# Expert rows scattered by choice and token in a two-layer diffusion trunk: stores, combination loads, gate rows and modulation moved between engines

## The reference

```python
DEPTH = 2; D_MODEL = 1024; SEQ = 128; DEC_SEQ = 512          # 640 tokens in all
N_EXPERTS = 32; TOP_K = 4; EXPERT_FF = 128; SHARED_FF = 256; ROUTE_SCALE = 2.5

def moe_ffn(h, p):
    t = h.reshape(-1, d)
    s = jax.nn.sigmoid((t @ p["w_router"]).astype(jnp.float32))
    _, idx = lax.top_k(s + p["b_router"].astype(jnp.float32), TOP_K)
    sel = jnp.take_along_axis(s, idx, axis=-1)
    w = sel / jnp.sum(sel, axis=-1, keepdims=True) * ROUTE_SCALE
    gates = jnp.einsum("nk,nke->ne", w, jax.nn.one_hot(idx, N_EXPERTS))
    hg = jnp.einsum("nd,edf->nef", t, p["w_e_gate"])
    hu = jnp.einsum("nd,edf->nef", t, p["w_e_up"])
    routed = jnp.einsum("nef,efd->nd", jax.nn.silu(hg) * hu * gates[:, :, None], p["w_e_down"])
    shared = (jax.nn.silu(t @ p["w_s_gate"]) * (t @ p["w_s_up"])) @ p["w_s_down"]
    return (routed + shared).reshape(bn, l, d)

def trunk_layer(x, cvec, p, layer, ctx=None):
    mods = jax.nn.silu(cvec) @ p["w_ada"] + p["b_ada"]
    sh1, sc1, g1, sh2, sc2, g2 = jnp.split(mods[:, None, :], 6, axis=-1)
    h = rmsnorm(x, p["g_pre1"]) * (1.0 + sc1) + sh1
    ...                                    # differential attention, SSD scan, neighbourhood attention
    mix = (ga * (o_da @ p["w_br_da"]) + gs * (o_ssm @ p["w_br_ssm"]) + gn * (o_na @ p["w_br_na"])) @ p["w_out"]
    x = x + g1 * rmsnorm(mix, p["g_post1"])
    h2 = rmsnorm(x, p["g_pre2"]) * (1.0 + sc2) + sh2
    x = x + g2 * rmsnorm(moe_ffn(h2, p), p["g_post2"])
```

## Time and profile before

| | us |
|---|---|
| median of 3 runs | 2956.16 (2955.13 to 2956.25) |
| the profiled execution's own time | 2964.08 |
| its span | 2962.3 |
| granted TensorE clock, mean | 0.935 |
| DMA, mean | 153 GB/s, 452.96 MB |
| stores of `y` in both loops | 76 |

### The profile page before, as it was taken

One profiled execution on the slowest core, in us unless ns is written; L12 is line 12 of the kernel. 1 busy time (PEld: TensorE's weight loads), 2 busy tenths in 40 slices (PEclk: granted clock), 3 DMA queues, 4 the chain that ended last, 5 costly groups with the idle time before them and its releaser, 6 DMA issues. The chain is left out here.

```text
span 2962.3 us, 32617 instructions
## 1 busy us (share of the span) xinstructions
PE 2582.0 (87%) x11924; PEld 1666.3 (56%) x11924; DVE 980.1 (33%) x1955; ACT 605.9 (20%) x1362; POOL 348.0 (12%) x338
## 2 busy tenths in 40 slices
PE   4999969879999989999829998986999998899993
PEld 2445634456457645677615565545656764577771
DVE  1414301463006334222164242136301633522226
ACT  2221100340014012122132121025001401212221
POOL 0005100011001100111220150000200110011113
PEclk8999989999988999999969999989998999999997
DMA  8441086100542030799853101710033103089996
GB/s 307 143 143 36 29 313 245 36 1 29 187 143 48 29 111 36 289 378 380 304 193 123 64 29 36 294 64 1 29 127 95 42 29 118 29 331 379 378 350 219
DMA packets 189030, 452.96 MB, mean 153 GB/s; under 512 B 30732, under 2 KB 52340, under 8 KB 188916
## 3 DMA queue, kind: packets, MB, share of 16 engines
q1 hardware_dynamic: 139668, 306.49, 29.1%
q10 hardware_dynamic: 31968, 82.02, 7.4%
q0 software_dynamic: 17280, 62.92, 5.8%
HBM read 362.00 MB, written 89.39 MB: 152 GB/s over the span
## 5 line engine op out<-in xcount | busy, mean ns | idle before, releaser
L221 PE MATMUL ps<-hT,ring 128*128 128x512 f32 x896 | 414.4, 617 | 13.7 <-PEq L2756 12.4
L2262 PEld LDWEIGHTS ps<-mixT,ring 128*128 128x128 f32 x2496 | 284.5, 192 | 96.9 <-issue 96.9
L2262 PE MATMUL ps<-mixT,ring 128*128 128x128 f32 x2496 | 297.1, 277 | 35.7 <-PE ps L2278 34.0
L221 PEld LDWEIGHTS ps<-hT,ring 128*128 128x128 f32 x896 | 173.2, 198 | 233.3 <-issue 233.1
L230 PE MATMUL ps<-ring,hT 128*128 128x512 f32 x480 | 212.3, 600 | 8.4 <-PEq L1177 7.4
L1215 POOL TENSOR_TENSOR mix_S<-ring 128x512 f32<-128x512 f32 x16 | 25.2, 1577 | 1197.5 <-POOLq L1352 630.3
L2148 PE MATMUL ps<-ring,mixT 128*128 128x512 f32 x320 | 144.0, 611 | 21.6 <-PEq L2756 21.6
L230 PEld LDWEIGHTS ps<-ring,hT 128*128 128x128 f32 x480 | 91.3, 192 | 122.5 <-issue 120.3
L2278 PE MATMUL ps<-ring,ex_hid 128*128 128x512 f32 x304 | 149.5, 614 | 0.0
L1264 PE MATMUL ps<-late,ring 128*128 128x320 f32 x512 | 144.4, 440 | 5.6 <-PEq L1701 2.5
L1264 PEld LDWEIGHTS ps<-late,ring 128*128 128x128 f32 x512 | 98.0, 193 | 49.8 <-issue 10.9
(11 more groups left out here) (404 smaller groups left out, 3605.0 us busy)
## 6 DMA issues: line engine op xcount, KB each, us to landing
ring<-in_w_e_gate SPq DMA_DIRECT2D x78, 512.0 KB
ring<-in_w_e_up SPq DMA_DIRECT2D x78, 512.0 KB
ring<-in_w_e_down SPq DMA_DIRECT2D x78, 512.0 KB
y_rows<-out_gpost ACTq DMA_DIRECT2D x76, 512.0 KB, 6.3
ring<-in_w_in SPq DMA_DIRECT2D x18, 2048.0 KB, 8.4
y_rows<-hT SPq DMA_DIRECT2D x12, 2560.0 KB, 31.1
ring<-in_w_gate SPq DMA_DIRECT2D x12, 2048.0 KB, 9.7
mixT<-in_w_ada ACTq DMA_DIRECT2D x8, 2048.0 KB, 9.4
```

What stands on the lines that cost most here:

```text
L221: pe.matmul(lat, wide[:, k, c], hT[:, k, CTX:TOK], start=(k == 0), stop=(k == kt_n - 1))
L2262: ins = pe.matmul(ps[:, 2 + b, g * P:(g + 1) * P], ew[:, k, :], xT[:, b, k, :], start=(k == 0), stop=(k == KT - 1))
```

## The change

Each result row now goes to a place of its own, choice x 640 + token, and rows of empty slots are not written. POOL scatters them with an indirect DMA in the loop; ScalarE's store is gone, and so are the filler stores and their wait. The gather leaves out empty slots too (an index beyond the bound). The table is therefore built from choice and token, and split on VectorE into `m.table` (the row to read) and `m.dest` (the row to write). Two small scatters of two rows each go into spare rows first and count for `y_stored`.

In the combination the rows are plain loads of 128 consecutive rows, issued by SP. The first row of each token goes through TensorE: `diag`, the identity scaled by the gate, times the row, added to the shared product in PSUM; VectorE adds the other three. The gate rows are loaded by ScalarE's queue near the start of the expert loop, the next layer's mods by SP at the start of `stage_tail`. ScalarE modulates all eight blocks.

```diff
@@ stage_da, sync: the filler stores
-            spare = UNROLL * (MAX_TURNS - MIN_TURNS)
-            for a in range(0, spare, TILES):
-                n = min(TILES, spare - a)
-                sp.dma_start(cx.y_rows[UNROLL * MIN_TURNS + a:...], cx.hT ...).then_inc(sem("rows_filled"), 16)
@@ stage_tail, sync
             load_mods(cx, sp, L, 1, mods, sem("mods_in"))
+            if L + 1 < DEPTH:
+                load_mods(cx, sp, L + 1, 0, m.mods, sem("co_mods_in"))
@@ stage_tail, gpsimd
                 pool.indirect_dma_start(xg[:, b, :], None, cx.h_rows,
-                                        bass.IndirectOffsetOnAxis(ap=index[:, b:b + 1], axis=0)).then_inc(...)
+                                        bass.IndirectOffsetOnAxis(ap=index[:, b:b + 1], axis=0), bounds_check=TOK - 1,
+                                        oob_is_err=False).then_inc(sem(f"xg_ready{b}"), 16)
+            def scatter(n, i):
+                b = n % 2
+                pool.wait_ge(sem("y_low"), at(n + 3, i))
+                pool.wait_ge(sem("y_high"), at(n + 3, i))
+                pool.tensor_copy(goal[:, b:b + 1], m.dest[:, bass.ds(at(n, i), 1)]).then_inc(sem("goal_ready"), 1)
+                pool.wait_ge(sem("goal_ready"), at(n + 1, i))
+                pool.sem_inc(sem("pool_go"), 1)
+                pool.indirect_dma_start(cx.y_rows, bass.IndirectOffsetOnAxis(ap=goal[:, b:b + 1], axis=0), y[:, b, :],
+                                        None, bounds_check=TOP_K * TOK - 1, oob_is_err=False).then_inc(
+                    sem(f"y_stored{b}"), 16)
             pool.wait_ge(sem("table_known"), 1)
+            for b in range(2):
+                pool.indirect_dma_start(cx.y_rows, bass.IndirectOffsetOnAxis(ap=goal[0:2, b:b + 1], axis=0), y[0:2, b, :],
+                                        None).then_inc(sem(f"y_stored{b}"), 16)
             gather(0)
             gather(1)
             with pool.Fori(0, count) as i:
                 for n in range(2, UNROLL + 2):
                     gather(n, i)
+                    scatter(n - 2, i)
+            for b in range(2):
+                pool.wait_ge(sem(f"y_stored{b}"), count * (16 * UNROLL // 2) + 16)
@@ stage_tail, scalar
             turned(0)
             shared(1)
+            act.wait_ge(sem("table_known"), 1)
+            act.wait_ge(sem("rows_stored"), 16 * TILES)
+            load_gate(cx, act, L, 1, m.gpost, m.gbias, m.ggain, sem("co_gains"))
             silu_up(0)
...
-                    act.wait_ge(sem("y_low"), at(n + 2, i))
-                    act.wait_ge(sem("y_high"), at(n + 2, i))
-                    act.dma_start(cx.y_rows[bass.ds(at(n - 1, i), 1)]..., y[:, b, :]).then_inc(sem(f"y_stored{b}"), 16)
@@ stage_tail, vector: what the table holds
-                                            token[:, t:t + 1], ALU.is_equal, ALU.mult)
+                                            place_of[:, n:n + 1], ALU.is_equal, ALU.mult)
-                dve.scalar_tensor_tensor(out=m.slot_of[:, k, :], ...)
-            dve.tensor_copy(m.table[:, :], ps[:, 3, 0:TABLE]).then_inc(sem("table_known"), 1)
+            known = ps[:, 3, 0:TABLE]
+            for b in range(2):
+                dve.tensor_scalar(goal[:, b:b + 1], col, float(TOP_K * TOK + 2 * b), None, ALU.add)
+            dve.tensor_scalar(tab[:, 0, :], known, 0.0, NO_ROW, ALU.is_equal, ALU.mult)
+            step(dve, dve.tensor_scalar(tab[:, 2, :], known, float(TOK), None, ALU.is_gt))
+            for k in range(2, TOP_K):
+                step(dve, dve.scalar_tensor_tensor(out=tab[:, 2, :], in0=known, scalar=float(k * TOK), ...))
+            step(dve, dve.scalar_tensor_tensor(out=tab[:, 1, :], in0=known, scalar=-1.0, in1=tab[:, 0, :], ...))
+            dve.scalar_tensor_tensor(out=m.table[:, :], in0=tab[:, 2, :], scalar=-float(TOK), in1=tab[:, 1, :], ...)
+            dve.tensor_copy(m.dest[:, :], tab[:, 1, :]).then_inc(sem("table_known"), 1)
@@ stage_combine
-        @block.gpsimd
-                pool.indirect_dma_start(yg[:, n % BUFS, :], None, cx.y_rows..., m.slot_of[:, k, t:t + 1] ...)
...
+                n = t * TOP_K
+                if t == 0:
+                    pe.wait_ge(sem("co_diag"), 1)
+                pe.wait_ge(sem(f"yg_ready{n % BUFS}"), 16 * (n // BUFS + 1))
+                for h in range(2):
+                    ins = pe.matmul(ps[:, 2 * (t % 3) + h, :], diag[:, t, :], yg[:, n % BUFS, h * SEC:(h + 1) * SEC],
+                                    start=False, stop=True)
...
-                for k in range(4):           # ScalarE; blocks 4 to 7 were VectorE's modulate(t), now gone
+                for k in range(KT):
...
-            load_gate(cx, sp, L, 1, gpost, old[:, 3, :], old[:, 4, :], sem("co_gains"))
+            def load_rows(t):
+                for k in range(TOP_K):
+                    n = t * TOP_K + k
+                    if n >= BUFS:
+                        sp.wait_ge(sem("yg_used"), n - BUFS + 1)
+                    sp.dma_start(yg[:, n % BUFS, :], cx.y_rows[k * TOK + t * P:k * TOK + (t + 1) * P, :]).then_inc(...)
+            load_rows(0)
+            load_rows(1)
             if more:
-                load_mods(cx, sp, L + 1, 0, mods, sem("co_mods_in"))
                 load_section(cx, sp, L + 1, 0)
             for t in range(TILES):
+                if t + 2 < TILES:
+                    load_rows(t + 2)
                 sp.wait_ge(sem("x2_ready"), t + 1)
...
+            for t in range(TILES):
+                ins = dve.tensor_scalar(diag[:, t, :], cx.ident, m.gates[:, 0, t:t + 1], None, ALU.mult)
+            ins.then_inc(sem("co_diag"), 1)
...
-                for k in range(TOP_K):
+                for k in range(1, TOP_K):
@@ trunk
-    cx.y_rows = nc.dram_tensor("y_rows", [UNROLL * MAX_TURNS, P, D], F32, kind="Internal").ap()
+    cx.y_rows = nc.dram_tensor("y_rows", [TOP_K * TOK + 4, D], F32, kind="Internal").ap()
```

More of the change, by code:

```diff
@@ L58 @@
 TABLE = UNROLL * MAX_TURNS + 4
+NO_ROW = 4096.0
 OFF = {}
@@ L2023, in sb @@
             return st.enter_context(nc.sbuf_tensor(f"{name}_{L}", shape, dt))
-        xn = sb("out_xn", [P, TILES, D])
+        xn = m.rest
         mods = Mods(sb("out_mods", [P, 184]))
@@ L2030, in stage_tail @@
         br = sb("route_br", [P, NE])
-        iota = sb("route_iota", [P, P + TILES + 1])
+        iota = sb("route_iota", [P, P + N_CHOICE + 1])
         s = sb("route_s", [P, TILES, NE])
@@ L2055, in stage_tail @@
         y = gpost
+        m.gpost = cx.late[:, :, :].rearrange("p a b -> p (a b)")[:, 0:2 * D].rearrange("p (g d) -> p g d", g=2)
+        m.gbias, m.ggain = m.rest[:, 0, :], m.rest[:, 1, :]
         row = iota[:, 0:P]
-        token = iota[:, P:P + TILES]
-        col = iota[:, P + TILES:P + TILES + 1]
+        place_of = iota[:, P:P + N_CHOICE]
+        col = iota[:, P + N_CHOICE:P + N_CHOICE + 1]
         block = st.enter_context(nc.Block())
@@ L2504, in _ @@
             for k in range(TOP_K):
-                dve.scalar_tensor_tensor(out=m.slot_of[:, k, :], in0=chosen[:, k, 1, :], scalar=float(P),
-                                         in1=chosen[:, k, 0, :], op0=ALU.mult, op1=ALU.add)
                 dve.tensor_copy(m.gates[:, k, :], chosen[:, k, 2, :])
@@ L2509, in _ @@
             dve.wait_ge(sem("table_mm"), 1)
-            dve.tensor_copy(m.table[:, :], ps[:, 3, 0:TABLE]).then_inc(sem("table_known"), 1)
+            known = ps[:, 3, 0:TABLE]
[4 more added lines that the diff above has]
+            for k in range(2, TOP_K):
+                step(dve, dve.scalar_tensor_tensor(out=tab[:, 2, :], in0=known, scalar=float(k * TOK), in1=tab[:, 2, :],
+                                                   op0=ALU.is_gt, op1=ALU.add))
+            step(dve, dve.scalar_tensor_tensor(out=tab[:, 1, :], in0=known, scalar=-1.0, in1=tab[:, 0, :], op0=ALU.add,
+                                               op1=ALU.add))
+            dve.scalar_tensor_tensor(out=m.table[:, :], in0=tab[:, 2, :], scalar=-float(TOK), in1=tab[:, 1, :],
+                                     op0=ALU.mult, op1=ALU.add)
+            dve.tensor_copy(m.dest[:, :], tab[:, 1, :]).then_inc(sem("table_known"), 1)
             def turned(n, i=0):
@@ L2527, in _ @@
             dve.sem_inc(sem("y_high"), 2)
-            for b in range(2):
-                dve.sem_inc(sem(f"y_stored{b}"), 16)
             dve.wait_ge(sem("experts_known"), 1)
@@ L2557, in stage_combine @@
         fs = sb("co_fs", [P, 6, TILES])
-        gpost = sb("co_gpost", [P, 2, D])
-        mods = Mods(sb("co_mods", [P, 184]))
+        gpost = m.gpost
+        diag = m.rest[:, 2, 0:TILES * P].rearrange("p (t q) -> p t q", q=P)
         spare = cx.ring[:, 1:SLOTS, :].rearrange("p s n -> p (s n)")
@@ L2563, in stage_combine @@
         block = st.enter_context(nc.Block())
-        @block.gpsimd
-        def _(pool):
-            for n in range(N_CHOICE):
-                t, k = n // TOP_K, n % TOP_K
-                if n >= BUFS:
-                    pool.wait_ge(sem("yg_used"), n - BUFS + 1)
```

(17 more changed lines are left out.)

43 lines of the change are left out of this document (14 added, 29 removed).

## The result

The changed kernel took 2935.19 us (median of 4 runs, 2934.94 to 2938.14) beside 2956.2 for the kernel before (4 runs), a ratio of 0.9938 (95% interval 0.9918 to 0.9959): 21.0 us less, where 41.9 were forecast. Later, beside the last experiments, it took 2942.28 (12 runs, 2930.68 to 2950.22) beside 2952.56 (17 runs), 0.9962 (0.9948 to 0.9977): 10.3 us less. All runs together have 2938.4 (16) against 2952.4 (63), so 14.0 us. The forecast of 2914.3 was wrong, and its range ended at 2935. The profiled execution of after took 2938.14 (span 2936.3).

A forecast was written before the change was run, and what follows sets the result against it. TensorE, busy 2582.0 of 2962.3 us, bounds the kernel; edits pay where it stands still or another engine ends a stage. -25.2 - 13.4 - 12.7 + 3.2 + 1.0 + 5.2 = -41.9, so 2956.2 becomes 2914.3 us; range 2904 to 2935.

The forecast's parts named there:

- Filler stores gone: Layer 0's differential attention: without SP's filler stores the ada loads land sooner, gain 25.2 us; layer 1 nothing.
- Layer 0's combination: Combination stage of layer 0: earlier first row and one row operation fewer, ScalarE then the bound, gain 12.7 us.
- 13.1 + 1.2 + 1.3 - 2.9 = 12.7: Layer 0's gain: earlier first row, three tiles at 0.4, tile 0's row operation, less doubled modulation in the last two.
- Layer 1's combination: Combination at the kernel's end: first row 7.5 us earlier, one row operation fewer per tile, gain 13.4 us.
- It fits, barely: Layer 1's combination: tile 3's rows, issued when tile 0 is finished, take about 8.4 us and arrive in time.
- Rival (d): Combinations bound by SP's loads or TensorE's twelve passes: 12 and 3 us less gain, 2929 us; chance 0.16.
- Expert loop: 76 tiles in both layers: gather behind the scatter in POOL's queue, landing taken as 5.0 us, cost 1.0 us.
- no wait, except for the few full tiles: Expert loop: gathers have 6.9 us to land and were taken to need 5.0, so TensorE hardly waits.
- Rival (a): Expert loop: gathers late behind scatters, mean landing 7.5, period 7.15, 21 us lost, 2935 us; chance 0.14.
- Rival (b): Expert loop: bounded indirect DMAs take POOL 2 us, gathers land 8.0 later, 116 us lost, 3029 us; chance 0.04.
- Block boundary: End of each tail block: POOL's last scatter and 3.3 us drain delay the next block, cost 2.6 us twice.
- Loop start: Before each expert loop: table operations and two small scatters delay the first gather, cost 1.6 us twice.

The follow-up runs named there:

- Early rows alone: Changed kernel with SP issuing the rows of tile t+3 ahead of its wait for x2_ready(t), TensorE's order kept: 2933.49 us.
- all four edits: Changed kernel plus transposes one tile behind products, rows issued earlier by SP, gather ahead of scatter, a DRAIN per loop trip: 2905.03 us, 0.9845.
- the modulation back: Kernel with all four edits, layer 0's combination modulated again by ScalarE (four blocks) and VectorE (four): 2897.89 us, 0.9817.

## Why the prediction was wrong

*Filler stores gone.* Right, in mechanism and size (25.2 forecast, 25.5 read, 24.6 given back when they were restored). It is the whole of the gain and more.

*Layer 0's combination: the step that failed.* It said "13.1 + 1.2 + 1.3 - 2.9 = 12.7" and read the stage as a race of VectorE against ScalarE. The first row is where it said (S+9.3 for S+9.6), and the tile's period, once ScalarE runs, is 1506.36 - 1497.21 = 9.15 for 9.1. What was not asked is what now stands ahead of `turn_norm(0)` in TensorE's queue. The order of that queue is not in the diff's minus or plus lines. All products came first before as well, but they needed only data that lay in SBUF and a PSUM buffer that VectorE had freed, and the `diag` product gave the fifth of them a wait for a row whose load needs tile 1 finished. Early rows alone gave 6.1 us, and early rows with the products one tile ahead of the transposes 11.2. The 12.7 were thus there to be had, and a queue order that the sum put at nothing held them. That ScalarE then sets the pace was read right: with the queue mended, giving four modulations back to VectorE gained 7.1 us.

*Layer 1's combination.* The first row came at S+8.0, as said. "It fits, barely" did not fit: rows waited 5.3 us in two tiles, and 2.5 us of the 13.4 are missing; early rows gave 2.0 back. Rival (d) named SP's order for both layers at 3 us a tile; it saw the right place in SP's queue, and missed that in layer 0 the wait delays all transposes. Its TensorE half, twelve passes at 8.1 us a tile, did not come: 3.60 and 1.88 us a tile where it did not wait.

*Expert loop: a term mis-sized, nearly as large.* It said "no wait, except for the few full tiles" and charged 1.0. The start was right: 2 x 0.9 of gap and 2 x 1.04 of DMA put the gather 7.0 us after its turn (forecast 6.8). But 6.9 us to land is no margin over a distribution of 2.1 to 8.8 with a median of 6.6: 13 waits, 11.6 us. I sized the landing at 5.0 by bytes, against the row of 6.3 in hand; the rows per gather did fall, and the landing rose to 6.6. Rival (a) had this mechanism at 21 us; a mean period was the wrong form for it, since only slow landings cost. Rival (b) did not come: an indirect DMA with bounds takes 1.03 to 1.04 us, not 2.

The Trainium skill's rule on software-generated DMAs starved by VectorE (SBUF — State Buffer, "SBUF: two separate sides") changed nothing here in what POOL takes to issue one: 1.032 us in the median for the scatters in the loop.

*Block boundary.* It said "drain 3.3": it took POOL's drain for a constant, and it is 0.082 us for each of 76 and 84 indirect DMAs instead of 38 and 42. That is +6.6 in the two, which the last scatters' quick landing partly paid back: 3.2 and 2.1 us instead of 4.5.
By the Trainium skill (DMA: Bandwidth & Descriptors, "Anatomy of one DMA") I had estimated 2.6 for that landing; the two rows lie on either side of it.

*Loop start.* 3.2 forecast, nothing lost: `turn(0)` did not wait for its gather. `gather(0)` did come later, 6.1 us ahead of the first `turn` instead of 9.6, near the 4.0 that the sum charged. But it landed in 4.3 us, where the sum had 6.3 to 8.0. No run shows why it was quick, and the zero is in part luck.

The ledger's missing 26.7 us are then: loops 12.1, layer 0's combination 13.2, boundaries 2.8, layer 1's combination 2.5, less 3.6 at the loop start and 0.3 at the ada loads.

## What to carry to other kernels

When an edit gives an instruction a new operand, walk down that engine's queue: everything behind it inherits the wait, even in lines that the diff does not show, and the operand's load must then be issued by when the queue gets there, not by when the old user wanted it. On an in-order queue with two kinds of work, issue first what is released first: moving one gather ahead of a scatter was worth 13 us of loop time here. Size a wait by the spread of its rows, not by one typical landing, and compare edits of a few us by the stretches that hold them, not by the whole time, and only after the same stretch has been read in several traces.

## What the runs showed of the hardware

*POOL's DRAIN at the end of these blocks grows with its indirect DMAs.* 38 and 42 of them since the last drain: 3.16 and 3.49 us; 76 and 84: 6.26 and 6.92; 77 and 85, with one gather more: 6.34 and 7.01; with 24 more: 8.23 and 8.87; the last scatter alone: 0.13. The combination of the kernel before, with 20 gathers, lies on the same line:

```profile
L2551 POOLq DRAIN  x2: 1685/1688/1691, 1522.2 to 2941.1; - x2
```

Right behind a gather, a drain in the loop took up to 9.75 us. In blocks without indirect DMAs drains of 0.3 to 4.0 us stand as well, those of 2.5 and 4.0 beside POOL's last computations. That the loop's drain takes over the work of the one at the end is inferred from the 0.13; what POOL does in it, the traces do not show.

*The granted clock in one stage differs between executions of equal work.* Layer 1's neighbourhood attention took 171.4 to 173.9 us in eight of the fourteen traces, 178.3 in one and 181.9 to 182.0 in five. The step is a stretch at the lower level in the middle of the stage. With all four edits:

```profile
2240.00:2304.00 64.00, 57.52 (x481) 50.06 (x482) 45.14 (x163) 41.41 (x122) 0.00 (x0) 1.00 0.41 100
```

and with the modulation back, an edit in another stage:

```profile
2234.00:2309.00 75.00, 69.11 (x482) 60.38 (x483) 45.31 (x163) 41.88 (x122) 0.00 (x0) 0.82 0.35 85
```

Of the two levels, 1.00 is 2.4 GHz throughout; 0.82 is a mean with a stretch at 1.2. In these 64 and 75 us it is 11 us, over the whole stage 10.5 between these two kernels and 8.0 between before and after. In layer 0 the same stage took 189.2 to 199.9 us, 199.9 in the kernel before and also in the one with the gather ahead of the scatter. Each step is of the size of an edit here. What decides it was not tried, and the kernel before was profiled once, so a part of the change in it is not excluded.
